# Moving the activation buffers to other start addresses and projecting q, k, v with 512-wide matmuls

## The reference

```python
for l in range(DEPTH):                       # 2 layers
    h = rmsnorm(x, pre_mix_g[l])
    z = h @ w_in[l]                          # 1024 x 2560: q | k | v (512 each), u | g (512 each)
    q = partial_rotary(q, positions); k = partial_rotary(k, positions)
    attn = dilated_mixture_attention(q, k, v)          # 8 heads x 64
    rec = jax.nn.gelu(g) * rg_lru(causal_dwconv(u, ...), ...)
    mixed = jnp.concatenate([rmsnorm(attn, ...), rmsnorm(rec, ...)], axis=-1)
    x = x + rmsnorm(mixed @ w_out[l], post_mix_g[l])
    h = rmsnorm(x, pre_ffn_g[l])
    f = swiglu(h, ...) if l % 2 == 0 else moe_ffn(h, ...)   # dense 3584, or top-2 of 8 experts of 3584
    x = x + rmsnorm(f, post_ffn_g[l])
```

## Time and profile before

| | before |
|---|---|
| median of 3 runs | 1522.08 us (1519.85 to 1527.04) |
| profiled execution, its own time | 1524.51 us |
| profiled execution, span | 1522.3 us |
| TensorE matmul busy (PE) | 1461.3 us, 96% |
| weight loads busy (PEld) | 1253.0 us, 82% |
| VectorE busy | 1187.6 us, 78% |
| ScalarE busy | 1016.1 us, 67% |
| DMA | 458.25 MB, mean 301 GB/s |
| mean granted TensorE clock | 0.963 of full speed |

### The profile page before, as it was taken

One profiled execution on the slowest core, in us unless ns is written; L12 is line 12 of the kernel. 1 busy time (PEld: TensorE's weight loads), 2 busy tenths in 40 slices (PEclk: granted clock), 3 DMA queues, 4 the chain that ended last, 5 costly groups with the idle time before them and its releaser, 6 DMA issues.

```text
span 1522.3 us, 21782 instructions
## 1 busy us (share of the span) xinstructions
PE 1461.3 (96%) x7620; PEld 1253.0 (82%) x7620; DVE 1187.6 (78%) x1311; ACT 1016.1 (67%) x1202; POOL 31.0 (2%) x54
## 2 busy tenths in 40 slices
PE   7998999999899799999999999999999999999993
PEld 7987999999798588888888888888888888888882
DVE  7856545455775678889889889889889988989886
ACT  6645444344464467787787787788778778779774
POOL 0001000000100110000000000000000000000001
PEclk9969999999995899999999999999999999999997
DMA  9604684445440379999999999999999999999993
GB/s 366 235 26 164 259 322 182 180 169 201 169 175 9 130 288 386 367 359 405 371 353 398 380 345 404 379 359 388 379 364 389 378 364 386 387 370 366 387 376 125
DMA packets 68477, 458.25 MB, mean 301 GB/s; under 512 B 9424, under 2 KB 9552, under 8 KB 15696
## 3 DMA queue, kind: packets, MB, share of 16 engines
q1 hardware_dynamic: 61200, 437.19, 74.5%
q10 hardware_dynamic: 6080, 16.26, 2.8%
q0 software_dynamic: 1152, 4.19, 0.8%
HBM read 442.40 MB, written 15.20 MB: 301 GB/s over the span
## 4 chain that ended last, share of the span: by engine, by line
PE 95%; DVE 2%; DMA 1%; ACT 1%; POOL 0%; issue 0%; SPq 0%; ACTq 0%
PE psum L448 30%; PE psum L450 30%; PE psum L449 30%; PE psum L720 2%; PE psum L582 1%; PE psum L706 0%; PE psum L534 0%; ACT lru_b L800 0%; PE psum L592 0%; PE psum L593 0%; PE psum L698 0%; DVE xs L1115 0%; DMA con<-consts 0%; DVE hn L1113 0%; DMA hn<-y_rows,dest_i 0%; PE psum L591 0%
## 5 line engine op out<-in xcount | busy, mean ns | idle before, releaser
L1013 DVE TENSOR_TENSOR w_lo<-ring,w_hi 128x1024 fp32r<-128x1024 f32 x819 | 950.8, 1220 | 124.4 <-ACT w_hi L787 123.5
L787 ACT ACTIVATE w_hi<-ring 128x1024 fp32r<-128x1024 f32 x819 | 816.2, 1053 | 137.3 <-PE psum L450 130.3
L448 PE MATMUL psum<-w_hi,hT_hi 128*128 128x512 f32 (+1 forms) x1152 | 436.0, 378 | 0.0
L450 PE MATMUL psum<-w_hi,hT_lo 128*128 128x512 f32 (+1 forms) x1152 | 430.4, 374 | 0.0
L449 PE MATMUL psum<-w_lo,hT_hi 128*128 128x512 f32 (+1 forms) x1152 | 429.7, 373 | 0.0
L450 PEld LDWEIGHTS psum<-w_hi,hT_lo 128*128 128x128 f32 x1152 | 217.8, 189 | 39.0
L449 PEld LDWEIGHTS psum<-w_lo,hT_hi 128*128 128x128 f32 x1152 | 218.3, 189 | 37.2
L448 PEld LDWEIGHTS psum<-w_hi,hT_hi 128*128 128x128 f32 x1152 | 218.2, 189 | 36.9
L448 PE MATMUL psum<-w_hi,act_hi 128*128 128x512 f32 x560 | 222.2, 397 | 0.0
L449 PE MATMUL psum<-w_lo,act_hi 128*128 128x512 f32 x560 | 221.5, 396 | 0.0
L450 PE MATMUL psum<-w_hi,act_lo 128*128 128x512 f32 x560 | 221.5, 395 | 0.0
(11 more groups left out here) (206 smaller groups left out, 753.3 us busy)
## 6 DMA issues: line engine op xcount, KB each, us to landing
ring<-moe_gate SPq DMA_DIRECT2D x114, 1024.0 KB, 6.6
ring<-moe_up SPq DMA_DIRECT2D x114, 1024.0 KB, 7.1
ring<-moe_down SPq DMA_DIRECT2D x112, 1024.0 KB, 7.0
ring<-in_units SPq DMA_DIRECT2D x20, 1024.0 KB, 8.3
ring<-dense_gate SPq DMA_DIRECT2D x14, 1024.0 KB, 5.1
ring<-dense_up SPq DMA_DIRECT2D x14, 1024.0 KB, 4.8
ring<-dense_down SPq DMA_DIRECT2D x14, 1024.0 KB, 4.9
ring<-out_units SPq DMA_DIRECT2D x8, 1024.0 KB, 5.7
```

The lines of the kernel that those rows point to most:

```text
L448: pe.matmul(dst, s_hi, m_hi, start=start, stop=False)
L450: return pe.matmul(dst, s_lo, m_hi, start=False, stop=stop)
L787: act.activation(w_hi[:, h % AHEAD, :], ring[:, n % RING, (h % 2) * HCOLS:(h % 2 + 1) * HCOLS], ACT.Copy).then_inc(hi_ready, 1)
L1013: dve.tensor_tensor(w_lo[:, h % AHEAD, :], ring[:, (h // 2) % RING, (h % 2) * HCOLS:(h % 2 + 1) * HCOLS], w_hi[:, h % AHEAD, :].bitcast(F3 ...
```

## The change

`u_pad` and `ones` change their places in the list of tensors, and the unit layout and the matmuls of q, k and v change. In the built program `act_hi` then begins at byte 204,928, a multiple of 128; so do `lru_y` to `lru_g`, `act_lo`, `blocks`, `ones`, `con` and also `u_pad` in its new place. `tokens` takes units of half the contraction by 512 columns, so that each of its matmuls is 128x512 and writes a whole bank; a half unit then holds two blocks of the contraction in place of four of half the width.

```diff
@@ build: SBUF tensors
         qk = sb("qk", [P, TT, 2 * AW])
-        u_pad = sb("u_pad", [P, LJ, T + TAPS - 1])
         lru_y = sb("lru_y", [P, LJ, T])
...
         blocks = sb("blocks", [P, 2, LJ, P])
+        ones = sb("ones", [P, P])
         con = sb("con", [P, NCON])
...
-        ones = sb("ones", [P, P])
...
         pair_gate = sb("pair_gate", [P, 2, TT])
+        u_pad = sb("u_pad", [P, LJ, T + TAPS - 1])
@@ tokens
-            def tokens(n, bank, at, halves=(0, 1)):
+            def tokens(n, bank, i, halves=(0, 1)):
                 for s in halves:
                     pe.wait_ge(lo_ready, 2 * n + s + 1)
-                    w = cols(half_at(2 * n + s), 0, FC, FC)
+                    w = cols(half_at(2 * n + s), 0, EC, EC)
                     for tt in range(TT):
-                        for k in range(4):
-                            mm = product(ps[bank + tt][:, at * FC:(at + 1) * FC],
-                                         hT(4 * s + k, tt * P, (tt + 1) * P), w(k),
-                                         start=(s == 0 and k == 0), stop=(s == 1 and k == 3))
+                        for k in range(2):
+                            kk = 4 * i + 2 * s + k
+                            mm = product(ps[bank + tt], hT(kk, tt * P, (tt + 1) * P), w(k),
+                                         start=(kk == 0), stop=(kk == DK - 1))
                     mm.then_inc(half_done, 1)
@@ host layout
-        "in_units": columns_in_units(a["w_in"]),
+        "in_units": keep(np.concatenate([columns_in_half_units(a["w_in"][:, :, :3 * AW]),
+                                         columns_in_units(a["w_in"][:, :, 3 * AW:])], axis=1)),
```

## The result

The changed kernel takes 1508.99 us (median of 4 runs, 1507.25 to 1510.88) against 1520.96 us before on the same chip (4 runs, 1518.62 to 1527.04). The ratio is 0.9914, 95% interval 0.9892 to 0.9936: 13.1 us less, with 9.7 to 16.4 in the interval; the medians lie 12.0 us apart. The forecast was 15.8 us, and a median of 1506. The profiled execution after took 1507.25 us, its span is 1505.2 us.

A forecast was written before the change was run, and what follows sets the result against it. The prediction took the distances between TensorE's matmul starts as the bound. Its terms, 10.3 + 2.0 + 3.5 = 15.8 us, less from the profiled 1524.5 us gave 1508.7, as a median 1506 us; range 1500 to 1517.

The forecast's parts named there:

- What bounds the kernel: TensorE in the changed stages: each nanosecond between two matmul starts is a nanosecond of the kernel; TensorE busy 96%.
- Term 1 (experts): Experts' down: 1344 matmuls lose 6.6 ns each, 8.9 us, plus 1.4 us from slow matmuls behind them; 10.3 us.
- The part for settling: Experts: six matmuls behind each down run lose their slowness, 0.03 us a run, 48 runs, 1.4 us.
- Term 2 (dense down): Dense part's down: 336 matmuls lose 7.0 ns each, 2.4 us, less about 0.3 in narrow matmuls; 2.0 us taken.
- Term 3 (q, k, v): q, k, v: 576 narrow matmuls become 288 wide, 3.8 us less, minus 0.3 for restarts; 3.5 us taken.
- +-1.7 us a layer: Attention at half clock: a stretch's length differs by 3.4 us between layers, costing 1.7 us; put into the range.
- The step that failed: Down against projection and gate: 6.6 ns a matmul put down to the stationary operand starting 64 bytes past a 128-byte multiple.
- The rule: SBUF read in 16-byte lines: a start at a multiple of 64 equals one of 128, leaving only q, k, v's gain.
- The first rival: Start address is not the reason: down stays at 233.3 ns, gain 3.5 us, time 1518.6 us; chance 14%.
- the second: Weight stream becomes the bound in the experts, which gain nothing; time 1516.6 us; chance 5%.
- The slower side: TensorE's clock: more attention time at half clock makes the kernel over 0.5% (7.6 us) slower; chance 4%.
- The scores' 1.8 us: Attention scores: if operand start addresses cost time, 16 heads would gain 1.8 us; value taken 0.

The follow-up runs named there:

- the starts alone: Kernel before with only the tensor order changed, giving the changed kernel's start addresses; q, k, v stay narrow: 1510.28 us against 1519.58, ratio 0.9939.
- the wide q, k, v alone: Kernel before with only `tokens` and `in_units` changed to 512-wide q, k, v matmuls: 1520.56 us, ratio 1.000; timed again 1521.95 us, ratio 1.000.

## Why the prediction was right in its numbers, and where its reason was not

**What bounds the kernel** was right: each nanosecond between starts counted, and no wait took its place.

**Term 1 (experts)** was forecast at 10.3 us and is 8 x 1.19 = 9.5 in the trace. Down came to 226.7 ns, and the slow six behind it went. The part for settling was a little too large.

**Term 2 (dense down)**: 2.0 us forecast, 1.7 in the trace, with the small loss in the narrow ones as expected.

**Term 3 (q, k, v)**: 3.5 us forecast. The stage between the gates and the sums of squares became 1.53 us shorter in each layer, and the two pieces behind it about 0.15 and 0.1, which is 3.6 in all. In the kernel's time it doesn't show: alone it gave 0, with +-1.9 and +-2.3 us, in two measurements of 12 runs.

**The sum** of the traces is 14.8 us; timed were 13.1 and 11.2 by the ratios. For the starts alone it is 11.2 traced, 9.3 timed, and for the wide q, k, v alone 3.6 traced, nothing timed. So 1.7 to 3.6 us are missing each time.

One profile of a kernel can't tell where they are, but every timed run has its mean granted clock on record. Of full speed it was 0.966 on average in the 34 runs of the kernel before that stand beside these kernels, 0.963 in the 24 runs of the wide q, k, v alone, 0.963 in the 5 of the starts alone, and 0.962 in the 10 of the changed kernel, of which none is above 0.963 (of the 34, 24 are at 0.965 or more). With two levels of the clock, half and full, the time at half clock is twice the span times what the mean lacks of 1: 103 us before, and 112, 110 and 115 in the other three. The 9 us more of the wide kernel cost at most half of their length, 4.7 us, and the changed kernel's 12 us at most 6: enough to cover what is missing. Compared at one clock, the gain of q, k, v comes out: at 0.965 and 0.966 the kernel before takes 1520.0 us (8 runs) and the wide one 1517.1 (7), at 0.962 and 0.963 it is 1524.0 (7) and 1521.7 (7), so 2.9 and 2.3 us less. So the record puts the missing gain down to half clock.

The prediction had "+-1.7 us a layer" for the clock, of either sign, in its range and nothing in its sum, while each kernel with faster matmuls that was timed several times had the lower clock. Why these kernels spend more time at half clock is not shown.

The 17.1 us between the two profiled spans are not the gain either: 2.1 of them lie ahead of layer 0's gates of the recurrence, where nothing was changed (40.44 before, 38.38 after, in the chain), and the profiled execution before, at a clock of 0.963, was one of the slower ones of its kernel.

**The step that failed** is the one with which the prediction called itself an inference: "So I put the 6.6 ns down to the start of the stationary operand." The 6.6 ns are right and come from the address, but not from a start off a multiple of 128, and not from the stationary operand by itself. Everything 64 bytes off is as fast; act at a multiple of 256 beside a w 128 past one is slow. What counts is how the pair lies modulo 256 bytes. The exclusion had left out that `hT` and `w` were alike in one more respect, their distance. The change worked because `act` and `w` came to the same place modulo 256 (both 128 past a multiple), and not because they came to a multiple of 128. So that terms 1 and 2 came true was luck: with `act` at the next multiple of 128 the rule of the prediction would have been kept, and down would have stayed at 5.59 us.

**The rule** of the Trainium skill (SBUF — State Buffer, "Specifications (TRN2)", lines of 16 bytes) speaks of one access and not of two operands. All starts here were multiples of 32, and the distances of starts still went from 226.7 to 233.3 ns; so by these runs it doesn't cover the case. The first rival (the address is not the reason) fell with the starts alone, the second (the stream of weights) with an item of 118.51 us, at which SP's queue still waited 340 times and 866 us for a free slot. The slower side did not occur. The scores' 1.8 us did not come either: from ScalarE's first work on the heads (line 894, at 83.71 and 79.85) to the transposes of line 622, both kernels take the same time in layer 0 (35.85 us before and 35.84 after in the chain).

## What to carry to other kernels

Read a matmul's cost from the distance of starts, by kind and by the tensors that it reads. Where two kinds of equal shape differ by 3%, the address is one candidate, and a pad of 64 bytes ahead of one of the two tensors shows whether it is. For streams of fp32r matmuls like these, each with a new stationary operand, lay out the stationary and the moving tensor of the 512-wide ones at the same place modulo 256 bytes, and of the 256-wide ones the moving tensor 32 or 64 bytes behind; an alignment of each by itself is neither needed nor enough. And for a change of under 0.3% trust the stage in the trace for the mechanism but not for the time: the clock moved this kernel by more. There, compare runs of equal mean granted clock.

## What the runs showed of the hardware that was not expected

- With two fp32r operands at the same place modulo 256 bytes a 128x512 matmul takes 226.7 ns at full clock; with the stationary one 32, 64 or 128 bytes behind it takes 232.9 to 233.3, and at 192 it takes 228.8.
- For 128x256 matmuls the same place is the slowest of those run: 119.9 ns, against 116.8, 117.8 and 118.6 with the moving operand 32, 64 and 128 bytes behind.
- Behind a run of slow matmuls the next six or so are slow, though these are of the fast kind (1.39 us for six against 1.36). Behind four transposes it is so in the changed kernel too: the 24 from 701.35 to 706.91 took 5.56 us, where 5.44 is the length of 24 undisturbed ones.
- The time of one kernel varies by 5 us and more between executions, with a granted clock that differs in the stretches around the norms. The kernels with the faster matmuls had the lower mean clock (0.962 and 0.963 against 0.966), and 1.7 to 3.6 us of what their stages gained are missing in their times.
